# A decoder layer on eight cores: routing table in two halves, gathers by quarters and ahead by a bias, the last expert by buckets, a planner with a longer DMA latency

## The reference

```python
hn = rmsnorm(x); proj = hn @ w_in                       # 2048 -> 4384 columns
h = x + concat(pool_mixer(proj[:, :1024]), rwkv7(proj[:, 1024:])) @ w_out
h = h + cross_attention(rmsnorm(h), rmsnorm(mem))       # 4 heads, 256 memory tokens
t = rmsnorm(h)
g_idx = argmax(t @ w_group); g_w = softmax(...)[g_idx]  # 1 of 4 groups
top_v, top_i = top_k(expert logits of that group, 2)    # 2 of its 4 experts
gates = softmax(top_v) * g_w
for e in range(16):                                     # SwiGLU, width 512
    h = h + gates[:, e] * (silu(t @ w_gate[e]) * (t @ w_up[e])) @ w_down[e]
out = rmsnorm(h)
```

## Time and profile before

| | |
|---|---|
| median of three runs | 2493.18 us |
| own time of the profiled execution | 2479.11 us |
| its span (slowest core, 7) | 2477.5 us |
| spans of the eight cores | 2448.7 to 2477.5 us |
| busy: PE, DVE, ACT, POOL | 2212.1, 1389.7, 1245.4, 394.9 us |

### The profile page before, as it was taken

The page is one execution under the profiler, slowest core; times in us unless marked ns, Lnnn a source line. Parts: engine busy times, 40 slices in busy tenths (PEclk is TensorE's granted clock), DMA queues, the critical chain, the costliest instruction groups (busy, mean ns, idle before and its releaser), DMA issues.

```text
span 2477.5 us, 57423 instructions; the slowest of 8 cores (2448.7 to 2477.5 us)
## 1 busy us (share of the span) xinstructions
PE 2212.1 (89%) x25144; PEld 1284.1 (52%) x25148; DVE 1389.7 (56%) x2607; ACT 1245.4 (50%) x2307; POOL 394.9 (16%) x655
## 2 busy tenths in 40 slices
PE   5888998999778899999997999999997698997996
PEld 3355555554445455555544455555554464555563
DVE  3455766677635567577775234333344565665755
ACT  6555775667646666666775332232332243223332
POOL 3222112111121212311010000000000111111111
PEclk9889999999889999999997999999998799998998
DMA  9877677775795887965675777877867588997893
GB/s 220 103 118 115 112 118 106 122 123 89 127 138 101 115 144 113 149 112 106 112 121 179 140 172 140 162 156 150 166 131 188 185 232 249 279 255 233 260 253 129
DMA packets 200704, 385.41 MB, mean 156 GB/s; under 512 B 81376, under 2 KB 135136, under 8 KB 188672
## 3 DMA queue, kind: packets, MB, share of 16 engines
q0 software_dynamic: 114000, 217.45, 55.4%
q1 hardware_dynamic: 86448, 164.23, 20.7%
HBM read 523.37 MB, written 134.35 MB: 265 GB/s over the span
## 4 chain that ended last, share of the span: by engine, by line
PE 74%; DMA 12%; DVE 5%; ACT 5%; issue 2%; POOL 1%; POOLq 0%; DVEq 0%; ACTq 0%
PE ps L133 74%; ACT big L156 5%; DMA big<-w_lo 3%; DVE big L163 3%; DMA big<-w_kv 2%; DVE big L168 2%; DMA big<-h_s,big 1%; DMA big<-wdc 1%; DMA big<-x 1%; DMA qkd<-big 1%; DMA vod<-big 1%; POOL big L198 1%; DMA big<-mem 1%; DMA out<-big 0%; DMA big<-w_qT 0%
## 5 line engine op out<-in xcount | busy, mean ns | idle before, releaser
L133 PE MATMUL ps<-big 64*64 64x64 bf16 (+6 forms) x25144 | 2212.1, 260 | 242.3 <-ACT big L156 77.5
L133 PEld LDWEIGHTS ps<-big 64*64 64x64 bf16 (+3 forms) x25144 | 1283.7, 109 | 1162.0 <-ACT big L156 155.0
L156 ACT ACTIVATE big<-ps 128x512 bf16<-128x512 f32 (+2 forms) x904 | 505.6, 588 | 778.5 <-PE ps L133 762.2
L163 DVE TENSOR_TENSOR big<-ps,big 128x512 bf16<-128x512 f32 (+3 forms) x656 | 465.0, 721 | 442.4 <-PE ps L133 313.7
L156 ACT ACTIVATE big<-big 128x512 f32<-128x512 f32 (+7 forms) x896 | 543.4, 632 | 247.1 <-DVE big L168 107.6
L168 DVE SCALAR_TENSOR_TENSOR big<-ps,big 128x512 f32<-128x512 f32 (+2 forms) x316 | 223.3, 721 | 145.2 <-ACT big L156 89.1
L156 ACT ACTIVATE big<-ps,big 128x512 f32<-128x512 f32 (+3 forms) x332 | 210.9, 647 | 185.2 <-PE ps L133 182.7
L168 DVE SCALAR_TENSOR_TENSOR big<-big 128x512 f32<-128x512 f32 (+4 forms) x212 | 228.1, 1080 | 29.7 <-DMA big<-h_s,big 17.4
L163 DVE TENSOR_TENSOR big<-big 128x512 bf16<-128x512 f32 (+11 forms) x412 | 202.1, 508 | 36.8 <-ACT big L156 29.1
L168 DVE SCALAR_TENSOR_TENSOR big<-big,ps 128x64 f32<-128x64 f32 (+1 forms) x280 | 92.8, 332 | 161.1 <-PE ps L133 157.5
L184 DVE CAST big<-ps 128x512 bf16<-128x512 f32 x168 | 111.1, 686 | 48.6 <-ACT big L156 30.7
(11 more groups left out here) (28 smaller groups left out, 258.5 us busy)
## 6 DMA issues: line engine op xcount, KB each, us to landing
big<-x SPq DMA_DIRECT2D x32, 1024.0 KB, 9.2
big<-w_rkv POOLq DMA_DIRECT2D x48, 512.0 KB, 9.5
wuc<-wu_l POOLq DMA_DIRECT2D x48, 512.0 KB, 9.2
wdc<-wd_l POOLq DMA_DIRECT2D x48, 512.0 KB, 8.6
wgc<-wg_l POOLq DMA_DIRECT2D x48, 512.0 KB, 7.7
big<-wuc SPq DMA_DIRECT2D x48, 512.0 KB, 10.8
big<-wgc SPq DMA_DIRECT2D x48, 512.0 KB, 10.2
big<-wdc SPq DMA_DIRECT2D x48, 512.0 KB, 7.9
```

The source lines that it names most:

```text
L133: r.append(e.matmul(out, lhsT=lhsT, rhs=rhs, start=st, stop=sp_, **k))
L156: return self.op("act", lambda e: e.activation(out=out, in_=in_, func=func, **kw), dur, R, W, P, tbl=TBL.get(func))
L163: return self.op(eng, lambda e: e.tensor_tensor(out=out, in0=a, in1=b, op=op), dur, R, W, P, after=after)
```

## The change

`DMA_LAT` becomes 5000. The temporaries of `routing` get a buffer each, and the operations of the gates stand behind those of the slots; `tab` is split into `tabi` (token number, used) and `tab` (both gates, factor), zeroed once and added to on DVE after each block's matmuls, which use any PSUM bank. `shapes` goes ahead of bucket 0's first transposes, at a point where PE has waited for `nmi` alone. In `gather` the norm, its buffer and its dependencies are cut into four quarters; the first three buckets use the six banks `eps_`; for buckets 0 to 5 ACT makes both copies of the first three quarters; and every operation of a gather gets the bias -30000, which counts as 30 us more of `bl`. The last expert's down projection goes bucket by bucket, and each bucket is finished as soon as its four blocks are added.

```diff
-DMA_LAT = 2000.0
+DMA_LAT = 5000.0
...
-        dur = 10.0 if pre is None else 2500.0
+        dur = 10.0
...
+        o = self.op("pe", fn, dur, R, W, P, mode=mode, **kw)
+        if pre:
+            o.pre = (pre[0], [pre[1].w] + pre[1].p)
+        return o
...
+            if o.pre:
+                for p in o.pre[1]:
+                    if p is not None:
+                        b.wait_ge(*p.tok)
+                o.pre[0](b)
             for s, v in waits[1:]:
                 b.wait_ge(s, v)
...
+GBIAS = -30000.0
...
-            dps = Ring(bank[0:7])
+            dps = Ring(bank)
-            tabp = bank[7].fresh()
+            S.memset(tab.a, 0.0, W=[tab])
+            S.memset(tabi.a, 0.0, W=[tabi])
...
-                S.red(gmax, lg, ALU.max, R_, W_)
-                S.tt(goh, lg, b3(gmax), ALU.is_equal, R_, W_)
-                S.tt(gsh, lg, b3(gmax), ALU.subtract, R_, W_)
-                S.act(gsh, gsh, AF.Exp, R_, W_)
+                S.red(gmax.a, lg, ALU.max, [lgb], [gmax])
+                S.tt(A(goh), lg, b3(gmax.a), ALU.is_equal, [lgb, gmax], [goh])
+                S.tt(t44, le, A(goh).unsqueeze(3).to_broadcast([128, 4, 4, 4]), ALU.mult, [lgb, goh], [t4])
+                S.red(A(esel), t44.rearrange("p t g e -> p t e g"), ALU.add, [t4], [esel])
...
-                for j in range(4):
-                    S.mm([(tabp.a[:, 0:120], ohr.a[:, j * 128:(j + 1) * 128], Fr.a[:, j * 120:(j + 1) * 120], bt == 0 and j == 0, bt == 3 and j == 3)],
-                         R=[ohr, Fr], P=[tabp])
+                for dst, f_, n in ((tabi, Fi, 48), (tab, Fr, 72)):
+                    b = dps.next()
+                    S.mm([(b.a[:, 0:n], ohr.a[:, j * 128:(j + 1) * 128], f_.a[:, j * n:(j + 1) * n], j == 0, j == 3) for j in range(4)], R=[ohr, f_], W=[b])
+                    S.tt(dst.a, b.a[:, 0:n], dst.a, ALU.add, R=[b, dst], W=[dst])
...
             def gather(b):
+                n0 = len(S.ops)
+                gather_ops(b)
+                for o in S.ops[n0:]:
+                    o.bias = GBIAS
...
-                S.stt(xn.fresh().a, y.a, tb[:, b, 4:5], gF.a, ALU.mult, ALU.mult, R=yq + [tab, gF], W=[xn])
+                for q in range(4):
+                    c = slice(q * 512, (q + 1) * 512)
+                    S.stt(xn.a[:, c], y.a[:, c], tb[:, b, 2:3], gF.a[:, c], ALU.mult, ALU.mult, R=[yq[q], tab, gF], W=[xnq[q]])
...
-                    pb = gps_.next()
+                    pb = (eps_ if b < 3 else gps_).next()
+                    fr = (b, q) == (0, 0)
...
-                        S.cp(dst[k][1][:, q * 4:q * 4 + 4], r3(pb.a, 4), R=[pb], P=[dst[k][0]], eng=("act", "dve")[k])
+                        S.cp(dst[k][1][:, q * 4:q * 4 + 4], r3(pb.a, 4), R=[pb], P=[dst[k][0]], eng="act" if k == 0 or b < 6 and q < 3 else "dve")
...
-                for db in range(4):
-                    w = piece(2, e, db)
+                for db, j in [(db, j) for db in range(4) for j in range(3)] if e < 15 else [(db, j) for j in range(3) for db in range(4)]:
+                    if db not in ws:
+                        ws[db] = piece(2, e, db)
...
+                    if e == 15 and db == 3:
+                        finish_bucket(b)
```

More of the change, by code:

```diff
@@ L31 @@
 class Op:
-    __slots__ = ("eng", "fn", "dur", "preds", "tbl", "bytes", "i", "start", "end", "bl", "bias", "tok", "clock", "succ", "n", "ready", "mode")
+    __slots__ = ("eng", "fn", "dur", "preds", "tbl", "bytes", "i", "start", "end", "bl", "bias", "tok", "clock", "succ", "n", "ready", "mode", "pre")
 class Buf:
@@ L1054, in routing @@
                 le = L[:, :, 4:20].rearrange("p t (g e) -> p t g e", g=4)
[L1055 to L1062, removed]
@@ L1083, in routing @@
[L1083 to L1090, removed]
+                gmax, gsum, gw, m1, m2, p1, p2, rk = [V(k, 4) for k in ("gmax", "gsum", "gw", "m1", "m2", "p1", "p2", "rk")]
@@ new lines, in routing @@
+                goh, gsh, esel, oh1, e2, ind, pe4, q4 = [V(k, 16) for k in ("goh", "gsh", "esel", "oh1", "e2", "ind", "pe4", "q4")]
+                t4, tok = V("t4", 64), V("tok", 4)
+                t44 = t4.a.rearrange("p (t g e) -> p t g e", t=4, g=4)
+                prs, plo, phi = [V(k, 24) for k in ("prs", "plo", "phi")]
+                sel, tmp, rnk = [V(k, 96) for k in ("sel", "tmp", "rnk")]
+                sel3 = A(sel)
+                S.red(gmax.a, lg, ALU.max, [lgb], [gmax])
+                S.tt(A(goh), lg, b3(gmax.a), ALU.is_equal, [lgb, gmax], [goh])
@@ new lines, in routing @@
+                S.op("dve", lambda e: e.reciprocal(out=p1.a, in_=p1.a), 100.0, [p1], [p1])
+                S.ts(p2.a, p1.a, -1.0, ALU.mult, 1.0, ALU.add, R=[p1], W=[p2])
+                S.tt(p1.a, p1.a, gw.a, ALU.mult, [p1, gw], [p1])
+                S.tt(p2.a, p2.a, gw.a, ALU.mult, [p2, gw], [p2])
+                S.tt(A(pe4), A(oh1), b3(p1.a), ALU.mult, [oh1, p1], [pe4])
+                S.tt(A(q4), A(e2), b3(p2.a), ALU.mult, [e2, p2], [q4])
+                S.tt(pe4.a, pe4.a, q4.a, ALU.add, [pe4, q4], [pe4])
@@ L1275, in shapes @@
                 one, w128, three = [es.enter_context(e.register(n)) for n in ("c1", "c128", "c3")]
-                r = [e.load(regs, nmi.a[0:1, :])]
+                e.load(regs, nmi.a[0:1, :])
                 for rg, v in ((one, 1), (w128, 128), (three, 3)):
@@ L1279, in shapes @@
                 for i in range(0, 16, 4):
-                    r.append(e.move_shape([e.shape_register(j) for j in range(i, i + 4)], [[(one, regs[j]), (w128, three), (one, one), (one, one)] for j in range(i, i + 4)]))
-                return r
+                    e.move_shape([e.shape_register(j) for j in range(i, i + 4)], [[(one, regs[j]), (w128, three), (one, one), (one, one)] for j in range(i, i + 4)])
             wxr = Ring([S.part(o_, 1024) for o_ in WP[:12]])
@@ L1288, in build @@
             XEr = Ring([e_.bf16(16 * 384) for _ in range(5)])
-            xn = e_.bf16(D)
+            xn, xnq = e_.bf16(D), [Buf() for _ in range(4)]
+            S.alias(xn, xnq)
             hidr = e_.bf16s(2, 4 * 384)
```

130 lines of the change are left out of this document (70 added, 60 removed).

## The result

The changed kernel takes 2457.64 us (median of four runs, 2446.63 to 2518.61) beside 2490.68 for the kernel before on the same chip; the ratio is 0.985, 95% interval 0.9804 to 0.9897. (The highest of the four, 2518.61, is a disturbed run; such runs stay in the medians given here, and the ratios leave them out.) The profiled execution took 2446.63, span 2445.1, on core 7, as in the profile before; that span is 32.4 shorter. The forecast was 2464, a gain of 29, with a range of 2445 to 2480.

A forecast was written before the change was run, and what follows sets the result against it. PE is busy nearly throughout dense stage 2, so only its idle time elsewhere can be won, with routing deciding the seam. Terms -16 + 2 - 2 - 6 - 7 = -29 take the median 2493.2 to 2464; range 2445 to 2480.

The forecast's parts named there:

- Routing: Seam: separate buffers take gate operations off the slot path and the slot matmuls are narrower; -5 us, range 1 to 6.
- The doubt: Routing: the planner puts gate operations between slot operations; at full step cost each, only about 1 us gain is left.
- Shapes and buckets: Seam, first gather to first expert: earlier register move -5 us and buckets by quarters -6 us, together -11.
- the move: Seam: loading row counts into PE's registers ahead of bucket 0 instead of bucket 1 gives 1 to 5 us, booked 5.
- the bucket edit: Seam: quarter norms, six banks and seven ACT copies a bucket give 6 us, range 0 to 10.
- Table in two halves: Dense stage 2: twice as many matmul passes of fewer columns cost 0 to 3.5 us more, booked +2.
- Mixer: Mixer, 100:620: planning with latency 5.0 removes most of PE's 8.7 us wait on `w_kv`; -7 us, bounds -30 to +20.
- a better plan cannot shorten that chain: Mixer, 620:840: PE waits 21.3 us on ACT, which waits for single-buffered x tiles; nothing booked.
- Experts: Experts: gather bias and longer planned hops cut gather and down-weight stalls; half of 12, -6 us, range -20 to +25.
- Tail: After the last matmul: last expert by buckets leaves fewer finishing passes; -2 us, range 0 to 4.7 gained.
- the caveat: Tail: a finishing pass that starts in a gap holds up the last bucket's accumulations by 2.34 us.
- Last matmul to last scatter under 7: Tail sign: last scatter issued under 7 us after the last matmul, against 8.7 before.

The follow-up runs named there:

- the three seam experiments: Changed kernel with whole bucket norm, old place of register move, or whole bucket edit undone; first gather to first expert matmul 20.05, 20.3 and 24.96 us.
- a_bank7: Changed kernel with stage 2's PSUM ring cut back to seven banks; median 2446.45 us, ratio 0.9774.
- a_tab1: a_bank7 with the routing table again one sum of 120 columns staying in the eighth bank; median 2438.41 us, ratio 0.9778.
- a_shapes1: Changed kernel with the register move ahead of bucket 1's transposes again; first gather to first expert matmul 20.3 us.
- a_nobias: Changed kernel with the gathers' priority bias at zero; median 2465.8 us, ratio 0.9849.
- a_lat2: Changed kernel planned with the old DMA latency of 2000 ns; median 2491.65 us, ratio 0.9966.
- a_whole: Changed kernel with a gathered bucket's norm as one operation of 2048 columns again; first gather to first expert matmul 20.05 us.
- a_seam: Changed kernel with whole norm, two banks and copies halved between ScalarE and VectorE, register move still ahead of bucket 0; first gather to first expert matmul 24.96 us.
- a_lat8: a_tab1 planned with a DMA latency of 8.0 instead of 5.0 us; median 2451.38 us, ratio 0.9839.
- a_dbmajor: Changed kernel with the last expert's accumulations in the old order, all three buckets per quarter of columns; last matmul to end 22.97 us.

## Why the prediction was right, and where not

**Routing: right** (-5 booked, -5.8; 9 to 11 us named, 9.0 measured). The doubt was that gate operations would stand between slot operations. They do, but an independent one costs about 0.1 from start to start (last section), not the 0.21 of the earlier trace rows, so the path hardly feels them, unless it is one that itself waits for PE, as in the three seam experiments. The matmul's share was over-reckoned: the halves give 0.7, not 1 and more.

**Shapes and buckets: right, and for the stated reasons** (-11 booked, -11.7; the move 4.9 of a booked 5, the bucket edit 6.8 of 6). ScalarE's seven copies a bucket do follow each other, as named. But the limit was mis-sized: 25 of them take 12.70 (1915.19 above), 0.51 each from start to start, not the 0.594 that the earlier trace rows give as the length of one, so three buckets take 10.7 of copies and not 12.6. What the sum did not have either is that the two edits overlap: undone singly each costs 2.

**Table in two halves: the term that failed.** Booked +2, "twice as many of fewer columns cost between 0 and 3.5 more". The passes were sized rightly (2.6), but the stage lost 16.2. Two things were left out: the dense stage was treated as PE's busy time plus passes, though a new plan there can open waits where PE had none (2.7 of them for the halves), and the eighth bank, which the same edit hands to the ring, changed the plan for 9.8 more, nearly all of it waits (12.8 to 3.7).

**Mixer: right mechanism, undersized** (-7 booked, -19.5). PE's waits on `w_kv` in 100:620 nearly vanished and came back with the old constant, as worked out. But the 8.7 of the earlier trace rows is the highest of eight cores; in the medians, 5.5 to 1.3, that wait gives 4 of the 19.5. Ten other kernels planned at 5.0 have mixers of 1387 to 1396, median 1391; against that the gain is about 15, and 4 or 5 of the 19.5 belong to this one profile. About as much is what all of PE's waits in 100:840, for engines and transfers, lost in the median of the cores: 75 before, 61 after, 73 with the old constant. One part of it contradicts the prediction: PE's waits on ScalarE in 620:840, where nothing was booked as "a better plan cannot shorten that chain", went from 18.3 to 14.9 in the median, and are 18.1 with the old constant. At 8.0 most of the gain was lost again. The Trainium skill, DMA: Bandwidth & Descriptors, section Anatomy of one DMA — SWDGE (gpsimd) path, speaks for the old 2.0. Here the landing of the earlier trace rows was the better guide for the planner.

**Experts: near in size, half by another way** (-6 booked, -11.1). The late down weights are gone, 12.1 to none, and the longest wait on a gather's norm fell from 9.45 to 2.9, as forecast. But waits on the silu's product rose. PE's waits there, after and then before (before's in 1948 to 2455):

```profile
PE ps L134 <- DVE big L168: 24.8, 16, 7.7
PE ps L134 <- DVE big L173: 8.1, 3, 2.9
PE ps L134 <- DVE big L189: 1.2, 2, 0.9
```

```profile
PE ps L133 <- DMA big<-wdc: 12.1, 2, 6.8
PE ps L133 <- DVE big L163: 11.3, 15, 4.3
PE ps L133 <- DVE big L168: 11.1, 4, 9.5
PE ps L133 <- ACT big L156: 3.3, 2, 2.6
PE ps L133 <- DVE big L184: 1.5, 3, 1.0
```

Before 39.3, after 34.1: 5.2 less, about the booked 6. The other 6 are busy time, 467.7 to 461.8, at a granted clock of 0.97 instead of 0.96; that the clock rose because fewer waits break the work up is argued, not shown. Nor can the 11.1 be shared out among edits: without the bias 7.0 are lost, with the old latency 6.2, with a whole norm 6.1, an edit that there touches only the gathers' norms, and these make more than the whole. The kernels that keep the changed kernel's order of the experts on VectorE and ScalarE (a_bank7, a_tab1, a_shapes1) have 490 to 493; of six with another order five have 497 to 500 (a_nobias, a_lat2, a_whole, a_seam, a_lat8) and one 493 (a_dbmajor). So nearly any other plan costs this stage 5 to 8, whatever edit called for it.

**Tail: the caveat came true** (-2 booked, -0.1). From the last matmul's end, 2422.22, to the last scatter it is 9.0 where the earlier trace rows have 8.7:

```profile
2411.69 10.53 PE L134 MATMUL ps<-big 128*128 128x512 bf16 x48 [0.65 <-DVE big L168]
```

```profile
2422.07 2.34 DVE L173 SCALAR_TENSOR_TENSOR big<-big 128x2048 f32<-128x2048 f32 x1
2424.32 0.75 DVE L173 SCALAR_TENSOR_TENSOR big<-ps,big 128x512 f32<-128x512 f32 x1
...
2431.18 0.98 POOL L1376 DMA_INDIRECT out<-big  x1 [0.27 <-issue]
```

A finishing pass of 2.34 stands between the last matmul and the last accumulation, as the text said it might. It should have been booked at nothing, and the sign "Last matmul to last scatter under 7" failed.

So the total is right partly by compensation: a loss of 14 that was not seen in stage 2 against some 18 more in mixer and experts. That these nearly cancel is luck; only the seam's terms were right one by one.

## What to carry to other kernels

Where a list scheduler sets the order, every edit is two: the edit, and a new plan; book the second wherever the edit touches a buffer ring, a constant or a priority, also in a stage where the bounding engine has no gap to lose. Before a wait is put into a sum, look at it on all cores: the slowest core's can be the highest of eight. A serial stretch on the critical path can be worked out from single rows, here to within a microsecond a term, but undo its edits together, since singly each hides behind the other. A removed stall in a packed stage tends to come back as another: look at what the next engine in line is doing before counting it.

## What the runs showed of the hardware

VectorE starts a small operation that doesn't need its forerunner's result before that one ends. From the routing of the changed kernel:

```profile
1905.77 0.16 DVE L168 TENSOR_TENSOR big<-big 128x4 f32<-128x4 f32 x1
1905.89 0.18 DVE L182 TENSOR_SCALAR big<-big 128x24 f32<-128x24 f32 x1
1905.98 0.16 DVE L192 TENSOR_REDUCE big<-big 128x4 f32<-128x12 f32 x1
```

0.12 and 0.09 from start to start, at 0.16 to 0.18 each. ScalarE's copies do the same: 0.51 from start to start in the seam, at 0.59 or more each. A matmul of f32 by 48 or 72 columns takes 272 and 269 ns, as one of 120 columns did (274): splitting a narrow one costs most of it again (6.1 of busy time against 3.5). A change of ScalarE's table costs 1.28 with the next operation 0.01 behind it (2067.81 to 2069.10 above). The Trainium skill, ScalarE: Activation LUTs, section What ACT_TABLE_LOAD costs, gives 1283 ns and a drain of some 1380 ns more. The first agrees, the second doesn't show in this trace.
